# GpSimd's norm operations in 256 columns instead of 1024, and layer 1's first gate-up piece split ahead of its norm

## What is computed

```python
for i in range(DEPTH):
    h = even_mixer(x, ...) if i % 2 == 0 else odd_mixer(x, ...)
    x = layer_norm(DN_ALPHA * x + h, ln_g[i, 0], ln_b[i, 0])
    x = layer_norm(DN_ALPHA * x + swiglu_ffn(x, ffn_w_gate_up[i], ffn_w_down[i]), ln_g[i, 1], ln_b[i, 1])

def layer_norm(x, g, b):
    xf = x.astype(jnp.float32)
    mu = xf.mean(-1, keepdims=True)
    var = jnp.square(xf - mu).mean(-1, keepdims=True)
    return ((xf - mu) * lax.rsqrt(var + LN_EPS) * g + b).astype(x.dtype)
```

## Time and profile before

| | us |
|---|---|
| median of 3 runs | 1213.73 (1213.05 to 1214.08) |
| the profiled execution | 1213.91 |
| its span, first to last instruction | 1212.0 |
| TensorE busy | 1102.2 (91%) |
| VectorE busy | 733.4 (61%) |
| ScalarE busy | 517.5 (43%) |
| GpSimd busy | 122.0 (10%) |

### The profile page before, as it was taken

How to read it: one execution, slowest core, us unless ns; L and a number is a source line. 1 busy time by engine, 2 the same in 40 slices (tenths; PEclk the granted TensorE clock), 3 DMA queues, 4 the chain that set the end, 5 groups by cost and what they waited for, 6 DMA issues and landing times.

```text
span 1212.0 us, 16898 instructions
## 1 busy us (share of the span) xinstructions
PE 1102.2 (91%) x7036; PEld 972.4 (80%) x7036; DVE 733.4 (61%) x1002; ACT 517.5 (43%) x734; POOL 122.0 (10%) x115
## 2 busy tenths in 40 slices
PE   5999899987999999789888599999879996999997
PEld 5788899865999988577666599998668775999885
DVE  3476875476766665745773666666565555666343
ACT  3452242253443433415763444343355655555331
POOL 1004653113000000400001200000010000000000
PEclk9897999888999999878999699999979997999999
DMA  9331002233877686234771777777434332555640
GB/s 288 103 122 70 1 1 71 70 129 111 304 252 240 219 309 242 81 131 157 104 220 35 232 254 244 252 237 283 165 106 139 105 105 69 175 175 190 194 171 35
DMA packets 113437, 193.67 MB, mean 160 GB/s; under 512 B 4658, under 2 KB 85057, under 8 KB 113234
## 3 DMA queue, kind: packets, MB, share of 16 engines
q1 hardware_dynamic: 109698, 179.66, 44.9%
q0 software_dynamic: 3248, 11.83, 4.3%
q10 hardware_dynamic: 416, 1.11, 0.2%
HBM read 188.39 MB, written 4.19 MB: 159 GB/s over the span
## 4 chain that ended last, share of the span: by engine, by line
PE 79%; DVE 12%; ACT 5%; issue 2%; SPq 1%; POOL 0%; DMA 0%; ACTq 0%; DVEq 0%
PE ps L415 22%; PE ps L416 21%; PE ps L417 21%; PE ps L1947 2%; PE ps L1932 2%; PE ps L1163 1%; DVE XL L548 1%; DVE ARR L399 1%; PE ps L1925 1%; PE ps L1173 1%; DVE STAT L565 1%; PE ps L1400 1%; DVE XN L562 1%; PE ps L1107 1%; PE ps L478 1%
## 5 line engine op out<-in xcount | busy, mean ns | idle before, releaser
L399 DVE TENSOR_TENSOR ARR<-ring,ARR 128x2048 fp32r<-128x2048 f32 (+1 forms) x143 | 320.4, 2246 | 212.4 <-ACT ARR L386 212.4
L415 PE MATMUL ps<-XH,ARR 128*128 128x256 f32 x1232 | 355.0, 288 | 26.9 <-DVE ARR L399 13.8
L386 ACT ACTIVATE ARR<-ring 128x2048 fp32r<-128x2048 f32 (+1 forms) x143 | 267.0, 1874 | 205.7 <-PE ps L417 155.2
L416 PE MATMUL ps<-XL,ARR 128*128 128x256 f32 x1232 | 352.0, 286 | 0.0
L417 PE MATMUL ps<-XH,ARR 128*128 128x256 f32 x1232 | 351.5, 285 | 0.0
L415 PEld LDWEIGHTS ps<-XH,ARR 128*128 128x128 f32 x1232 | 238.3, 193 | 32.1 <-issue 29.1
L416 PEld LDWEIGHTS ps<-XL,ARR 128*128 128x128 f32 x1232 | 238.6, 194 | 0.1
L417 PEld LDWEIGHTS ps<-XH,ARR 128*128 128x128 f32 x1232 | 238.3, 193 | 0.0
L415 PE MATMUL ps<-ARR 128*128 128x512 f32 x420 | 170.4, 406 | 8.4 <-DVE ARR L500 4.6
L417 PE MATMUL ps<-ARR 128*128 128x512 f32 x420 | 167.2, 398 | 0.0
L416 PE MATMUL ps<-ARR 128*128 128x512 f32 x420 | 167.1, 398 | 0.0
(11 more groups left out here) (336 smaller groups left out, 1280.9 us busy)
## 6 DMA issues: line engine op xcount, KB each, us to landing
ring<-in_ffn_w_gate_up_dram SPq DMA_DIRECT2D x44, 1024.0 KB, 5.7
ring<-in_w_dram SPq DMA_DIRECT2D x32, 1024.0 KB, 5.2
ring<-in_w_ada_dram SPq DMA_DIRECT2D x24, 1024.0 KB, 5.3
ring<-in_ffn_w_down_dram SPq DMA_DIRECT2D x22, 1024.0 KB, 5.1
ring<-in_even_w_in_dram SPq DMA_DIRECT2D x13, 1024.0 KB, 5.7
ring<-in_w_in_dram SPq DMA_DIRECT2D x9, 1024.0 KB, 5.3
ring<-in_mla_w_q_b_dram SPq DMA_DIRECT2D x6, 768.0 KB, 4.4
ring<-in_even_w_out_dram SPq DMA_DIRECT2D x4, 1024.0 KB, 4.8
```

Source lines behind the costliest of these rows:

```text
L386: e.activation(split(i)[0], raw(i), ACT.Copy).then_inc(*up("hi", ("hi", i)))
L399: e.tensor_tensor(lo, raw(i), hi.bitcast(F32), ALU.subtract).then_inc(*up("lo", ("lo", i), ("raw free", i)))
L415: e.matmul(out, lhs[0], rhs[0], start=first, stop=False)
L416: e.matmul(out, lhs[0], rhs[1], start=False, stop=False)
```

## The change

GpSimd's `pool_affine` (norms n0, n1 and n2) works through each 1024 columns in four operations of 256. All four multiplies come before the four adds, and the one wait between multiply and add stays. And ahead of `act_residual` and `dve_residual` of n2 stands a split through the piece behind `mout` 6, that is layer 1's first gate-up piece.

```diff
@@ pool_affine
             for t in range(2):
                 for step in xn_ready(i)(t):
                     e.wait_ge(*at(step))
-                e.tensor_tensor(X[:, t, :], XN[:, t, :], GB[:, 0, :], ALU.mult).then_inc(*up("affine"))
+                for o in range(0, D, 256):
+                    c = slice(o, o + 256)
+                    e.tensor_tensor(X[:, t, c], XN[:, t, c], GB[:, 0, c], ALU.mult).then_inc(*up("affine"))
                 e.wait_ge(*now("affine"))
-                e.tensor_tensor(X[:, t, :], X[:, t, :], GB[:, 1, :], ALU.add).then_inc(*up("affine", ("x", i, t)))
+                for o in range(0, D, 256):
+                    c = slice(o, o + 256)
+                    steps = [("x", i, t)] if o == D - 256 else []
+                    e.tensor_tensor(X[:, t, c], X[:, t, c], GB[:, 1, c], ALU.add).then_inc(*up("affine", *steps))
@@ scalar
             act_attend(e, MLA, act_beside_mla)
+            act_split(e, ahead("mout", 6, False) + 1)
             act_residual(e, 2)
@@ vector
             dve_attend(e, MLA, dve_beside_mla)
+            dve_split(e, ahead("mout", 6, False) + 1)
             dve_residual(e, "mout", 2, x_after(1))
```

## The result

The changed kernel takes **1203.63 us** (median of 4 runs, 1202.54 to 1205.01); the kernel before took 1213.49 (4 runs, 1213.05 to 1214.08). By the medians that is 9.9 us faster, where 14.3 were forecast; the ratio on record, which is not the one of the two medians (that would be 0.9919), is 0.9925 with a 95% interval of 0.9903 to 0.9947, or 9.1 us. A second set of 6 runs gave 1201.51 us and 0.9914 (0.9898 to 0.9929). The profiled execution took 1203.38 us, span 1201.5, so the two profiled spans differ by 10.5 us.

A forecast was written before the change was run, and what follows sets the result against it. TensorE has 79% of the chain, with VectorE's L548 held up by GpSimd behind the norms. Gains 6.8 + 2.7 + 2.7 + 2.1 = 14.3 us gave 1199.4 us, 8-in-10 range 1196 to 1203.5.

The forecast's parts named there:

- The step that failed: GpSimd behind the norms: next gains' loads issue some 1 to 3 us later, needed a whole stage later; no cost counted.
- Part 1, the split ahead: Layer 1, n2: splitting the first gate-up piece ahead of the residual makes layer 1 like layer 0, gaining 6.8 us.
- Its cover: Ahead of n2: the split fits VectorE's 5.87 us wait for TensorE, ending 2.3 us before that wait does.
- Part 2 at n0 and n2: 256-column GpSimd operations shorten L548's waits, so TensorE's uninterrupted work starts earlier: 2.7 us gained at each norm.
- Part 2 at n1: 256-column GpSimd operations bring TensorE's start and the second piece's L399 earlier: 2.1 us gained, between 1.2 and 2.8.
- A cover is gone in part: Rival, 0.12: L548's wait halves but returns at the norm's second half, clock comes up later; gain 10.4, 1203.3 us.
- The clock does more: Rival, 0.10: TensorE idles less and returns to 2.4 GHz sooner at all three norms; gain 17.6, 1196.1 us.
- The other three: Rivals: GpSimd still holds VectorE out (0.07, 1206.9 us); split ahead does nothing (0.04, 1206.2); slower, split waits (0.02).

The follow-up runs named there:

- experiment 1: Changed kernel, with GpSimd's four gain and gate row loads behind n0 and n2 held until step 20 of the gate-up loop: 1195.29 us, ratio 0.9853.
- experiment 11: Repetition of the changed kernel with all four GpSimd loads behind n0 and n2 held until step 20: 1194.91 us, ratio 0.9853.
- experiment 7: Kernel before, with three extra GpSimd writes ahead of its loads behind n0 and n2, so these go out later: 1211.16 us, one run.
- 4: Kernel before, with only GpSimd's four loads behind n0 and n2 held until step 20: 1212.93 us, ratio 0.9994.
- experiment 3: Changed kernel with GpSimd's operations back at 1024 columns, so only the split ahead remains: 1204.32 us, ratio 0.9931.
- experiment 6: Changed kernel with only the last two of GpSimd's four loads (1 MB) held until step 20: 1196.65 us, one run.
- 9: Changed kernel with 256 columns at n1 only, 1024 elsewhere, split ahead kept: 1199.84 us, one run.
- 2: Changed kernel without the split ahead, so only GpSimd's operations of 256 columns remain: 1206.23 us, ratio 0.9936.
- 5: Changed kernel measured again, nothing altered, beside other runs on the same chip: 1201.51 us, ratio 0.9914.
- 8: Changed kernel with 512 columns instead of 256 and all four GpSimd loads held until step 20: 1199.14 us, ratio 0.9885.
- 10: Changed kernel with 128 columns instead of 256 and all four GpSimd loads held until step 20: 1195.57 us, ratio 0.9854.

## Why the prediction was wrong, step by step

**The step that failed** is the one that priced GpSimd's later loads at nothing: "The loads of the next gains are issued some 1 to 3 us later and are needed a whole stage later." Both halves are true and the conclusion is not. It asked who needs these loads, not whom they share the DMA engines with. The rows gave GpSimd's end (297.87), the prediction itself moved it by 1 to 3 us, and it moved the second half of the norm (300.09 to 297.1), behind which stand the first splits and with them the ring load, 3 us the other way. So the trace of before (loads out from 298.43 to 300.06, ring load at 306.25) was enough to work out the meeting: about 301.4 to 303.1 against 303.3, where 301.46 to 303.09 and 303.10 were measured. The transfers of the moved steps were looked at one at a time and never laid over each other. It cost 3.2 to 3.5 us at n0 and 3.9 to 4.1 at n2 (experiments 1 and 11 against the changed kernel), 7.1 to 7.5 together; by the ratios, 0.9925 or 0.9914 against 0.9853, 7.4 to 8.7.

**Part 1, the split ahead** (forecast 6.8): right, with 7.5 measured. With it alone n2's distance fell by 7.5, to 87.82; both layers then have the same distance within 0.7 us, which was the argument. Its cover held: L562 waits 2.45 us for TensorE where 2.3 were worked out. TensorE starts on L548, and its wait there is 1.90 instead of 13.85.

**Part 2 at n0 and n2** (2.7 each): the mechanism was right and the local size a little low. The pairs of L548 take 1.95 us, where the prediction worked out 294.1 and 295.4 for the two ends (measured 294.3 and 295.3 from nearly the same start), and the uninterrupted work begins 3.0 us earlier. The clock came up as much earlier (near 303.1 instead of 306.5). Without the collision 3.4 to 3.6 us stay at n0 (88.53 against 84.94 and 85.17), and at n2 both parts together give 10.8 to 10.95 where 9.5 were forecast. In the changed kernel 0.14 stays at n0, and 6.9 of 9.5 at n2.

The Trainium skill's rule that the prediction drew on (SBUF — State Buffer, "Who interferes with whom"), that the loser waits for the whole instruction of the other, holds in all of these. The maximum of L548 goes with GpSimd's size, 2.85 us at 1024 columns, 1.76 at 512, 1.22 at 256 and 0.94 at 128: less the 0.69 of a free one, each time no more than one GpSimd operation (2.7, 1.25, 0.71 and 0.44).

**Part 2 at n1** (2.1, at most 2.8): too small for what the two profiles differ by, 46.14 - 42.54 = 3.6, but not for what the columns give. TensorE's first product behind n1, before and after:

```profile
503.31 0.77 PE L415 MATMUL ps<-ARR,XH 128*128 128x512 f32 x1 [2.92 <-DVE XL L548]
```

```profile
502.38 0.76 PE L415 MATMUL ps<-ARR,XH 128*128 128x512 f32 x1 [1.93 <-DVE XL L548]
```

Against the first L548 it starts 1.0 us earlier, and the 1.06 us that TensorE stood for L399 at 512.27 are gone: 2.1 us, as forecast. The rest is the clock. In both profiles it falls 30.5 us behind the first L548, when TensorE, which began later, has more left in the kernel before, and that runs at 0.50 of the clock. The distance with 1024 columns was 46.14 and 46.19, but 44.54 in experiment 7 and 43.83 in 4, where the granted clock fell 3 us later in cq's stretch, and it was 42.3 to 42.6 in every kernel with 256 and with 128. Why before and experiment 3 then stay low for 20 us, and the others for 17, is not settled.

**The ledger** between the two profiled spans: n0 0.14, n1 3.6, n2 6.88, all else -0.1, in all 10.5 of 14.3. What was lost to the collision, 7.1 to 7.5, was half made up by terms that came out larger than forecast: n0 and n2 without it by 1.9 to 2.3, n1 by 1.5. So the forecast missed by 4 us because an unforeseen loss and these gains partly cancelled; that it missed by no more is luck.

**The rivals.** "A cover is gone in part" had named 1203.3, and the time came out there, but not by its mechanism: the clock did not come later, and although L548 at the second half takes 1.99 us a pair instead of 1.29, TensorE's uninterrupted work still starts 3.0 us earlier. That the number agrees is luck. "The clock does more" (1196.1) is nearly what the kernel does once the loads are out of the way (1195). The other three did not occur. None of the rivals had two transfers meet.

## What to carry to other kernels

When an edit lets one engine go earlier and another finish later, lay the transfers that both issue over each other: a load that nobody needs for a long time is not free if it goes out in the few microseconds in which a needed one does. Bulk loads without a deadline can wait for a semaphore that comes later in the stage; here two lines brought 7 to 9 us on top of the 9 to 10 that the change had kept (1195 us, 1.5% faster than before). And test a gain at an anchor some tens of microseconds on, not at the wait that it removes: the 3 us at n0 were there at 297.85 and gone at 381.73.

## What the runs showed of the hardware

**A load is late by the bytes that another queue was asked for just before it.** A 1 MB load of SP's queue takes 5.1 us alone, 7.3 with 1 MB of GpSimd's queue issued 1.0 to 1.6 us ahead of it (experiment 6), 8.5 with 2 MB issued 3.4 to 5.0 us ahead (experiment 7), and 10.1 to 10.4 with 2 MB issued up to 1.6 us ahead (all behind n0), while the engines are busy for 0.9 and more of most stretches of 2 us and move some 300 to 410 GB/s in all three. The loads issued first are not much held up: the last of GpSimd's four lands after 7.9 us instead of 6.6. The Trainium skill says (DMA: Bandwidth & Descriptors, "Queues, rings and completion order") that each DMA engine takes turns between its queues by the packet. The trace of the changed kernel agrees only late in the meeting: from 308 to 309 us it has 81 packets of GpSimd's queue and 80 of SP's, but these carry 0.31 and 0.08 MB, so equal turns gave the ring load a fifth of the bytes. In the 4 us from the issue of the ring load (303.10) to 307 it has no packet of SP's queue at all, where in experiment 11 there are 30 within 1.4 us of the issue. Why SP's queue gets no turn in those 4 us was not found. No run shows either whether what the profile counts as a packet is the packet of that rule.

**The granted clock falls in some executions and not in others.** Between cq's low parts and n2 stand 119.3 us in the profiles of before, of the changed kernel, and of experiments 3, 9 and the repetition of 1, 120 to 121.5 in 2, 4, 5, 7, 8 and 10, and 122.8 or 122.9 in 1 and 6. In experiment 1 the clock is low twice for some 3.5 us in the attention, in the same stretch as in the repetition, where it is not (span, then busy times, granted clock, DMA share, GB/s):

```profile
575.00:578.00 3.00, 3.00 (x10) 2.38 (x9) 1.79 (x1) 0.66 (x2) 0.00 (x0) 0.63 1.00 103
```

```profile
578.00:581.00 3.00, 3.00 (x15) 2.43 (x14) 2.12 (x1) 1.46 (x5) 0.00 (x0) 1.00 0.96 101
```

The start varies likewise: n0's first L548, ahead of which these kernels differ only in GpSimd's operations of that norm, stands anywhere from 288.15 to 293.34. What sets off such a fall was not found.
